# Loading x in two halves on two queues, with other start-up loads held until it has landed

## What is computed

```
x   = [x_prompt (256 x 1024); x_sample (8 x 1024)]
z   = rmsnorm(x, ab_norm_g) @ ab_w_in          # layer 0, 3584 columns
q,k = rope(z[...]); mix = moba attention | retention; x += mix @ ab_w_out
x  += convffn(rmsnorm(x, ffn_norm_g[0]))       # uses ffn_conv_w, ffn_conv_b, state_ffn_conv
... layer 1: mLSTM and a second convffn; y = rmsnorm(x, final_norm_g)
```

## Time and profile before

| what | value |
|---|---|
| time, median of 3 runs | 958.67 us (957.46 to 960.42) |
| profiled execution, first to last instruction | 959.2 us |
| PE busy | 883.4 us, 92% |
| DVE busy | 622.1 us, 65% |
| ACT busy | 420.1 us, 44% |
| POOL busy | 257.4 us, 27% |
| moved by DMA | 159.83 MB, mean 167 GB/s |

### The profile page before, as it was taken

One profiled execution on the slowest core, in us unless ns is written; L12 is line 12 of the kernel. 1 busy time (PEld: TensorE's weight loads), 2 busy tenths in 40 slices (PEclk: granted clock), 3 DMA queues, 4 the chain that ended last, 5 costly groups with the idle time before them and its releaser, 6 DMA issues.

```text
span 959.2 us, 16875 instructions
## 1 busy us (share of the span) xinstructions
PE 883.4 (92%) x6145; PEld 761.0 (79%) x6145; DVE 622.1 (65%) x943; ACT 420.1 (44%) x695; POOL 257.4 (27%) x226
## 2 busy tenths in 40 slices
PE   2999894969999999999999999969969999999996
PEld 1988783742325999999999999857648999999995
DVE  3689988660032798888556656565476888887442
ACT  4434333341011565555545433564334655555442
POOL 6154767710100332232001000161221332222010
PEclk9999996588999999999999999975597999999997
DMA  9837675335565555554556667403353566653631
GB/s 275 284 129 242 199 260 183 128 94 160 192 220 175 176 177 175 178 184 129 172 177 192 191 187 216 161 10 100 88 155 93 171 192 188 188 157 121 183 119 46
DMA packets 154406, 159.83 MB, mean 167 GB/s; under 512 B 11793, under 2 KB 136349, under 8 KB 154335
## 3 DMA queue, kind: packets, MB, share of 16 engines
q1 hardware_dynamic: 145520, 151.09, 50.6%
q10 hardware_dynamic: 7966, 6.33, 2.2%
q0 software_dynamic: 864, 1.68, 0.7%
HBM read 150.76 MB, written 8.50 MB: 166 GB/s over the span
## 4 chain that ended last, share of the span: by engine, by line
PE 81%; DVE 11%; ACT 4%; issue 2%; DMA 2%; ACTq 0%; POOL 0%; SPq 0%; DVEq 0%
PE bank L1396 20%; PE bank L1397 20%; PE bank L1398 20%; PE bank L1604 6%; DVE w_lo L921 3%; DVE sc_all L973 2%; PE bank L1773 1%; PE bank L1726 1%; DMA z<-in_c_out_norm_g 1%; PE bank L1485 1%; PE bank L1600 1%; PE bank L1566 1%; PE bank L1748 1%; PE bank L1737 1%; DVE z L968 1%
## 5 line engine op out<-in xcount | busy, mean ns | idle before, releaser
L530 ACT ACTIVATE w_hi<-w_raw 128x1024 fp32r<-128x1024 f32 (+2 forms) x230 | 227.9, 993 | 297.8 <-PE bank L1398 294.5
L921 DVE TENSOR_TENSOR w_lo<-w_raw,w_hi 128x1024 fp32r<-128x1024 f32 (+2 forms) x230 | 296.1, 1289 | 83.6 <-ACT w_hi L530 83.4
L1396 PE MATMUL bank<-actB_hi,w_hi 128*128 128x264 f32 x704 | 200.1, 284 | 0.0
L1397 PE MATMUL bank<-actB_lo,w_hi 128*128 128x264 f32 x704 | 199.5, 283 | 0.0
L1398 PE MATMUL bank<-actB_hi,w_lo 128*128 128x264 f32 x704 | 199.3, 283 | 0.0
L1396 PE MATMUL bank<-actA_hi,w_hi 128*128 128x264 f32 x624 | 184.8, 296 | 5.8 <-DVE w_lo L921 2.9
L1397 PE MATMUL bank<-actA_lo,w_hi 128*128 128x264 f32 x624 | 180.1, 289 | 0.0
L1398 PE MATMUL bank<-actA_hi,w_lo 128*128 128x264 f32 x624 | 179.8, 288 | 0.0
L1397 PEld LDWEIGHTS bank<-actB_lo,w_hi 128*128 128x128 f32 x704 | 132.6, 188 | 0.1
L1396 PEld LDWEIGHTS bank<-actB_hi,w_hi 128*128 128x128 f32 x704 | 132.6, 188 | 0.1
L1398 PEld LDWEIGHTS bank<-actB_hi,w_lo 128*128 128x128 f32 x704 | 132.0, 187 | 0.0
(11 more groups left out here) (326 smaller groups left out, 1191.2 us busy)
## 6 DMA issues: line engine op xcount, KB each, us to landing
w_raw<-in_ffn_w SPq DMA_DIRECT2D x44, 1024.0 KB, 5.3
kv<-in_cache_k SPq DMA_DIRECT2D x64, 256.0 KB, 3.0
kv<-in_cache_v SPq DMA_DIRECT2D x64, 256.0 KB, 3.1
w_raw<-in_c_w_in SPq DMA_DIRECT2D x16, 1024.0 KB, 5.6
w_raw<-in_ab_w_in SPq DMA_DIRECT2D x14, 1024.0 KB, 5.4
w_raw<-in_ffn_w SPq DMA_DIRECT2D x16, 768.0 KB, 4.5
w_raw<-in_ffn_w SPq DMA_DIRECT2D x16, 640.0 KB, 4.1
w_raw<-in_ab_w_out SPq DMA_DIRECT2D x4, 1024.0 KB, 5.7
```

The source lines that it names most:

```text
L530: A(whi[u % RING][:, 0:nk, :], raw[u // 2 % RING][:, 0:nk, P * (u % 2):P * (u % 2) + P], ACT.Copy).then_inc(sem("hi_ready"), 1)
L921: V.tensor_tensor(wlo[u % RING][:, 0:nk, :], raw[u // 2 % RING][:, 0:nk, P * (u % 2):P * (u % 2) + P], whi[u % RING][:, 0:nk, :].bitcast(F ...
L1396: M(bank[b][:, 0:T], hi[:, k, :], src[0][:, k0 + k, :], start=first and k == 0, stop=False)
L1397: M(bank[b][:, 0:T], hi[:, k, :], src[1][:, k0 + k, :], start=False, stop=False)
```

## The change

x_prompt is loaded in two halves of 128 tokens, the first by ACT and the second by SP. SP also takes x_sample, and issues these and its three norm weights ahead of w0. POOL waits for `x_landed` (now ten loads) ahead of its convolution rows, states and copies, though not ahead of the page table. ACT waits for `x_landed` ahead of the large constants. SP's wait ahead of w1 and PE's wait count to ten.

```
+            sp.dma_start(x_tok[:, 1, :], x_prompt[0, P:TP]).then_inc(sem("x_landed"), 16)
+            sp.dma_start(xs_tok, x_sample.rearrange("b o n -> (b o) n")).then_inc(sem("x_landed"), 16)
+            for at, v in ((G_FFN, ffn_norm_g[0]), (G_FFN + 8, ffn_norm_g[1]), (G_FIN, final_norm_g)):
+                sp.dma_start(vec_rows[at:at + 8, :], v.rearrange("(k p) -> k p", p=P)).then_inc(sem("x_landed"), 16)
             for n in range(14):
                 load_raw(n, w_in0[:, :, 256 * n:256 * n + 256])
                 if n == 0:
-                    for at, v in ((G_FFN, ffn_norm_g[0]), (G_FFN + 8, ffn_norm_g[1]), (G_FIN, final_norm_g)):
-                        sp.dma_start(vec_rows[at:at + 8, :], v.rearrange("(k p) -> k p", p=P)).then_inc(sem("x_landed"), 16)
-
-                    sp.wait_ge(sem("x_landed"), 16 * 9)
+
+                    sp.wait_ge(sem("x_landed"), 16 * 10)
...
             pool.dma_start(pg[:], page_table.rearrange("(o b) n -> o (b n)", o=1)).then_inc(sem("pages_landed"), 16)
+            pool.wait_ge(sem("x_landed"), 16 * 10)
             for l in range(2):
...
-            act.dma_start(x_tok, x_prompt[0].rearrange("(t p) n -> p t n", p=P)).then_inc(sem("x_landed"), 16)
-            act.dma_start(xs_tok, x_sample.rearrange("b o n -> (b o) n")).then_inc(sem("x_landed"), 16)
+            act.dma_start(x_tok[:, 0, :], x_prompt[0, 0:P]).then_inc(sem("x_landed"), 16)
             for at, v, n in ((G_AB, ab_norm_g[0], 8), (G_RET, ab_ret_norm_g[0], 4), (G_C, c_norm_g[0], 8),
                              (G_OUT, c_out_norm_g[0], 8)):
                 act.dma_start(vec_rows[at:at + n, :], v.rearrange("(k p) -> k p", p=P)).then_inc(sem("x_landed"), 16)
+            act.wait_ge(sem("x_landed"), 16 * 10)
             act.dma_start(cst[:, C_COS:NCONST], consts[:, C_COS:NCONST]).then_inc(sem("const_landed"), 16)
...
-            pe.wait_ge(sem("x_landed"), 16 * 9)
+            pe.wait_ge(sem("x_landed"), 16 * 10)
```

## The result

The changed kernel takes 955.88 us (median of 20 runs, 951.58 to 963.91) and the kernel before 962.0 us (20 runs, 956.32 to 968.84): a ratio of 0.9948, with a 95% interval from 0.9926 to 0.9969. On 962 us that ratio is 5.0 us less, between 3.0 and 7.1; the two medians lie 6.1 us apart. The forecast was 3.7 us, 955.0 us.

The account below looks back on a forecast made before the run. Computation bounds most of the kernel, but loads bound its start: the first `w_hi` moves from 14.59 to 10.9 us, so 959.2 - 3.7 = 955.5 us span, 955.0 us median; range 952.6 to 958.6 us.

Parts of the forecast that it names:

- What bounds the start: Kernel start: nothing is computed until x and norm weights land; bound by bytes, PE's first instruction at 13.99 us before.
- w0 at 10.7 us, x at 8.7 us: Forecast landing times of the first weight chunk and of x, x taken midway between 7.8 and 9.6 us.
- the 2.36 MB of the sum: Bytes ahead of the first `w_hi`: x, x_sample, small constants, norm weights and w0, passed by 9.5 us.
- the estimate from the last byte to the semaphore: w0's landing: some 1.2 us assumed between its last byte, at 9.5 us, and its semaphore.
- The table load: ACT's 1.28 us load now follows its wait for x; 1.25 us of lost cover, mostly hidden by w0's landing.
- w0 as the wait: Rival at the start: w0 lands late, first `w_hi` at 12 to 13.3 us, about 956.7 us; chance 0.22.
- The bound of 13.3 us: Latest first `w_hi`: all 0.88 MB of constants pass ahead of w0's last byte, adding 2.6 us; gain 1.3 us.
- 7.51 us from the first `w_hi` to the second, called ACT's own work: After the first `w_hi`: ACT's stretch stays 7.51 us, so the gain there passes to everything behind.
- What is moved back costs nothing: Delayed w1 to w3, large constants and POOL's loads stay covered: 4 us for w1, 6.4 us for convolution rows.
- eaten by a later chunk: Rival after the start: a later weight chunk becomes the wait and takes the gain, about 958 us; chance 0.12.
- POOL too late: Rival at the convolution rows: POOL can't issue while DVE works, rows land at 35.8 us, 962.8 us; chance 0.06.
- the rule that the prediction names: Trainium skill, POOL's DMA issues: DVE's fp32 SBUF-to-SBUF copy locks GpSimd's descriptor writing out of a shared port.

Follow-up runs that it names:

- late start: Changed kernel, but PE's first instruction also waits for POOL's twelve convolution loads; 968.58 us in 9 runs, ratio 1.0067 to the kernel before.
- before again: The kernel before the change, unedited, profiled a second time; first `w_hi` at 14.46 us.
- changed again: The changed kernel, unedited, profiled a second time; first `w_hi` at 10.32 us.
- the order alone: Changed kernel without POOL's and ACT's waits for x, loads in the new order; first `w_hi` at 17.83 us, 3.2 us later than before.
- the waits alone: Kernel before plus only POOL's and ACT's waits for x, loads in the old order; first `w_hi` at 13.09 us against 14.59 us.
- the second kernel: Changed kernel without ACT's wait, large constants in 8 loads with rows of 856 bytes instead of one load; first `w_hi` at 12.39 us.

## Why the prediction was right

The time, 955.88 us, lies in the range, and the mechanism is the one that was forecast; the gain is 5.0 us instead of 3.7, the forecast within its interval. That the time lies so near the 955.0 us is luck: the forecast took 3.7 us from 958.67 us, the median of three runs, while 20 runs of the kernel before have 962.0 us. The base was 3.3 us too low and the difference of the medians, 6.1 us, 2.4 us larger than forecast, and the two nearly cancel.

- **What bounds the start.** Right: PE's first instruction comes when x and the norm weights are in, and the start is bound by loads. The late start shows that the end follows it.
- **w0 at 10.7 us, x at 8.7 us.** Measured 10.3 and 8.4 us. The bytes came out: the 2.36 MB of the sum had passed at 9.7 us, forecast for 9.5 us.

```profile
DMA packets 1639, 2.37 MB, mean 244 GB/s; under 512 B 154, under 2 KB 1375, under 8 KB 1639
```

  That is the DMA view of 0 to 9.7 us. The term that was too large is the estimate from the last byte to the semaphore, 1.2 us: w0 landed 0.6 us behind 9.7 us. SP issued w0 at 2.63 instead of 3.3 us, since half a load of x takes 0.40 us to issue, x_sample 0.37 and the three norm weights 0.91, instead of 0.60, 0.62 and 1.29 us; w0's sum does not use this time. For x the prediction took the middle between 7.8 and 9.6 us, with no row that spoke for it; that it came within 0.3 us is luck in part.
- **The table load.** Right: 2.02 us from 8.40 to 10.42 us, hidden except for 0.06 us, because w0 is as late. With the table load out of the way, 1.30 us of waiting for w0 stand bare. That the table load would be bare if w0 alone came earlier was not run; it follows from the rows, as `gains` ends at 10.33 us.
- **w0 as the wait.** Did not come, since nothing joined w0 in time. From 7 to 9.6 us the DMA view of the changed kernel has all of its 690 packets on SP's queue:

```profile
DMA packets 690, 0.69 MB, mean 267 GB/s; under 512 B 12, under 2 KB 690, under 8 KB 690
...
q1 hardware_dynamic: 690, 0.69, 91.2%
```

  The bound of 13.3 us behind this rival adds 2.6 us for the large constants ahead of w0's last byte; without ACT's wait they cost 2.5 us (12.86 against w0 at 10.36 us). It holds only while POOL waits: with both waits left out w0 landed at 17.8 us.
- **7.51 us from the first `w_hi` to the second, called ACT's own work.** Wrong. It is 6.82 us now, at 0.71 to 0.75 instead of 0.82 us for a tile, and 7.52 us again when PE and ACT start together in the late start. PE's transposes set that pace before; in the changed kernel PE starts 1.9 us ahead of ACT's `w_hi` instead of 0.6 us, because of the table load, and ACT goes at its own pace. That is 0.69 us more of gain, 4.86 us at the second `w_hi`. Two tiles before, where ACT follows PE at 0.82 us:

```profile
14.23 0.69 PE L1418 MATMUL bank<-cst,z 128*128 128x128 f32 x2
...
15.05 0.69 PE L1418 MATMUL bank<-cst,z 128*128 128x128 f32 x2
...
15.63 0.52 ACT L537 ACTIVATE actA_hi<-x,gains 128x264 fp32r<-128x264 f32 x1
...
16.45 0.52 ACT L537 ACTIVATE actA_hi<-x,gains 128x264 fp32r<-128x264 f32 x1
```

  and in the changed kernel:

```profile
11.39 0.50 ACT L540 ACTIVATE actA_hi<-x,gains 128x264 fp32r<-128x264 f32 x1
...
12.10 0.50 ACT L540 ACTIVATE actA_hi<-x,gains 128x264 fp32r<-128x264 f32 x1
```

- **What is moved back costs nothing.** Right: L1455 does not wait, the two last `w_hi` follow at once (2.94 us in one row) where ACT waited 1.15 us for w1 before. Nor was the gain eaten by a later chunk: the waits view of the whole execution has 1.1 us of `w_hi` behind a load before and none in the changed kernel.
- **From the second `w_hi` on.** 4.86 us of lead are 4.35 us at the sum of squares' end (`var` at 27.73 against 32.08 us). In the trace of the changed kernel PE's first unit runs its matmuls at 0.42 us until 23.0 us, 4.1 us after its first, and at 0.28 us behind; before, until 3.0 us after the first. They start 0.22 us and then 0.12 us apart, and 264 columns in 0.22 us are 1.2 GHz, the lower of TensorE's two levels. The windows view gives 1.00 there, but the trace's record of the granted clock only begins where the matmuls become faster: at 23.48 us in the changed kernel, at 27.18 us before. PE had idled 3.55 us ahead of this unit, 2.94 us before. The place differs from one execution to the next of the same kernel: in before again none of the 24 matmuls of the unit is faster than 0.42 us, and the record begins at 29.23 us, 5.6 us after the first; in changed again at 22.29 us, 3.5 us after. So these 0.5 us are no property of the change, as far as four executions tell; why the rise comes at different places is left open.
- **POOL too late.** Did not come: POOL's four issues of convolution states took 2.07 us while DVE worked, as long as before, and the eight of `state_ret` 6.01 us against 6.03:

```profile
8.29 6.03 POOL L381 DMA_DIRECT2D s<-in_state_ret  x8
```

  DVE's copies out of PSUM and its two-operand work do not disturb POOL's issues here. No copy within SBUF ran beside them, so the rule that the prediction names is not tested.

## What to carry to other kernels

When loads bound the start, list what the first computation needs, issue only that, and hold everything else by a wait: here the order alone lost 3.2 us at the first computation, the waits alone gave 1.5 us, and both together 4.2 us. A wait that is put ahead of a DMA issue also holds what stands behind it on that engine, such as a table load; look for it before the price is hidden by something that a later edit removes. Where one execution's time scatters by several us, read a change of 4 us from a row of the trace at the place where it acts, and show by a larger shift that this place reaches the end.

## What the runs showed of the hardware

Two queues that both had work were served about packet for packet, and so not by equal bytes: in 2.5 us a load with rows of 6848 bytes had 115 packets and 0.79 MB, one with rows of 1024 bytes 138 packets and 0.14 MB; against rows of 856 bytes it was 428 packets and 0.33 MB to 441 and 0.45 MB. A later stretch of the second kernel, with 803 to 418 packets, does not fit this and stays open. A queue can be well into the next load when the one ahead has not landed: without the two waits SP's queue had moved 0.3 MB beyond w0 by 17 us, and w0 had not landed. The time of one kernel differs by 12 us over 20 runs, and the slower runs are those at the lower mean granted clock (0.913 to 0.928 in the changed kernel).
